# Stage boundaries of a two-block network run in two halves of 256 tokens

## The reference

```python
def first_block(x, c, ...):                  # norms after each part
    for l in range(2):
        sh1, sc1, g1, ..., g3 = split(silu(c) @ w_ada[l] + b_ada[l], 9)
        y = swiglu(modulate(x, sh1, sc1), gate, up, down)       # width 2816
        x = layer_norm(ALPHA * x + 0.5 * (1 + g1) * y)
        y = token_mixer(modulate(x, sh2, sc2), w_in, w_out)
        x = layer_norm(ALPHA * x + (1 + g2) * y)
        y = swiglu(modulate(x, sh3, sc3), gate, up, down)
        x = layer_norm(ALPHA * x + 0.5 * (1 + g3) * y)

def second_block(x, mem, ...):               # norms before each part
    for i in range(2):
        x = x + (even_mixer, odd_mixer)[i](rmsnorm(x, g_mix[i]))
        x = x + cross_attn(rmsnorm(x, g_xattn[i]), rmsnorm(mem, g_mem[i]))
        x = x + relu(rmsnorm(x, g_mlp[i]) @ w_up[i]) ** 2 @ w_down[i]   # width 4096
```

## Time and profile before

| what | us |
| --- | --- |
| median of 3 runs | 3831.74 (3830.46 to 3831.81) |
| the profiled execution | 3830.17 |
| its span, first to last instruction | 3828.9 |
| PE busy in the span | 3560.9 |
| DVE, POOL, ACT busy | 1763.9, 1426.8, 1220.7 |
| mean granted clock of PE | 0.954 |

### The profile page before, as it was taken

One profiled execution on the slowest core, in us unless ns is written; L12 is line 12 of the kernel. 1 busy time (PEld: TensorE's weight loads), 2 busy tenths in 40 slices (PEclk: granted clock), 3 DMA queues, 4 the chain that ended last, 5 costly groups with the idle time before them and its releaser, 6 DMA issues.

```text
span 3828.9 us, 41108 instructions
## 1 busy us (share of the span) xinstructions
PE 3560.9 (93%) x16548; PEld 2879.4 (75%) x16548; DVE 1763.9 (46%) x3102; ACT 1220.7 (32%) x1650; POOL 1426.8 (37%) x721
## 2 busy tenths in 40 slices
PE   8999899899998999899799988988989998988999
PEld 7888667688877888667678866746868886777888
DVE  4444654654455444644531235685552224564222
ACT  2222362332223222542332223235342232343222
POOL 3343432333344334322343342212344444525443
PEclk9999899899998999898899989978999998999999
DMA  6333321133342444211122221100212222222222
GB/s 252 143 145 134 107 88 66 72 120 139 143 143 99 143 144 142 99 66 45 65 89 95 92 83 55 56 12 34 89 59 95 99 99 71 98 69 84 91 98 77
DMA packets 52609, 373.42 MB, mean 98 GB/s; under 512 B 5826, under 2 KB 5954, under 8 KB 9539
## 3 DMA queue, kind: packets, MB, share of 16 engines
q1 hardware_dynamic: 52418, 370.79, 26.9%
HBM read 368.67 MB, written 2.10 MB: 97 GB/s over the span
## 4 chain that ended last, share of the span: by engine, by line
PE 82%; DVE 11%; ACT 3%; issue 2%; POOL 2%; DMA 0%; DVEq 0%; ACTq 0%; SPq 0%; POOLq 0%
PE ps L1213 82%; ACT s_wh L1527 1%; DVE s_nu L1808 1%; DVE s_xr L1920 1%; DVE s_tmp L1846 1%; DVE s_tmp L1843 1%; PE ps L1233 0%; ACT s_hh L1527 0%; DVE s_wl L1833 0%; DVE s_tmp L2052 0%; POOL s_hl L2314 0%; ACT s_tmp L1659 0%; DVE s_tmp L2062 0%; POOL s_wl L2321 0%; DVE s_hl L1824 0%
## 5 line engine op out<-in xcount | busy, mean ns | idle before, releaser
L2321 POOL TENSOR_TENSOR s_wl<-s_stage,s_wh 128x1024 fp32r<-128x1024 f32 (+2 forms) x277 | 925.6, 3342 | 1401.3 <-ACT s_wh L1527 1401.0
L1213 PE MATMUL ps<-s_hh,s_wh 128*128 128x512 f32 (+1 forms) x2840 | 1137.8, 401 | 66.8 <-POOL s_hl L2314 45.6
L1213 PE MATMUL ps<-s_hl,s_wh 128*128 128x512 f32 (+1 forms) x2840 | 1119.9, 394 | 0.0
L1213 PE MATMUL ps<-s_hh,s_wl 128*128 128x512 f32 (+1 forms) x2840 | 1118.7, 394 | 0.0
L1527 ACT ACTIVATE s_wh<-s_stage 128x2048 fp32r<-128x2048 f32 (+1 forms) x277 | 519.7, 1876 | 715.3 <-PE ps L1213 684.4
L1213 PEld LDWEIGHTS ps<-s_hh,s_wh 128*128 128x128 f32 (+1 forms) x2840 | 541.4, 191 | 209.2 <-issue 79.0
L1833 DVE TENSOR_TENSOR s_wl<-s_stage,s_wh 128x1024 fp32r<-128x1024 f32 (+1 forms) x268 | 328.2, 1224 | 687.1 <-ACT s_wh L1527 687.1
L1213 PEld LDWEIGHTS ps<-s_hh,s_wl 128*128 128x128 f32 (+1 forms) x2840 | 540.6, 190 | 117.3 <-issue 0.2
L1213 PEld LDWEIGHTS ps<-s_hl,s_wh 128*128 128x128 f32 (+1 forms) x2840 | 541.9, 191 | 112.7 <-issue 2.1
L1213 PE MATMUL ps<-s_ah,s_wh 128*128 128x512 f32 x1216 | 475.3, 391 | 0.0
L1213 PE MATMUL ps<-s_ah,s_wl 128*128 128x512 f32 x1216 | 474.2, 390 | 0.0
(11 more groups left out here) (408 smaller groups left out, 3660.9 us busy)
## 6 DMA issues: line engine op xcount, KB each, us to landing
s_stage<-in_w_ada SPq DMA_DIRECT2D x64, 1024.0 KB, 4.8
s_stage<-in_ffn_w_gate SPq DMA_DIRECT2D x44, 1024.0 KB, 4.8
s_stage<-in_ffn_w_up SPq DMA_DIRECT2D x44, 1024.0 KB, 4.8
s_stage<-in_ffn_down SPq DMA_DIRECT2D x32, 1024.0 KB, 4.8
s_stage<-in_w_up SPq DMA_DIRECT2D x32, 1024.0 KB, 4.8
s_stage<-in_down_m SPq DMA_DIRECT2D x32, 1024.0 KB, 4.8
s_stage<-in_w_in SPq DMA_DIRECT2D x24, 1024.0 KB, 4.8
s_stage<-in_ffn_down SPq DMA_DIRECT2D x16, 768.0 KB, 4.3
```

Source lines behind the costliest of these rows:

```text
L1213: return pe.matmul(out, lhs, rhs, start=start, stop=stop, skip_group_check=True)
L2321: pool.tensor_tensor(m.WL[:, ws, 0:cut], m.STAGE[:, j % NS, 0:cut], m.WH[:, ws, 0:cut].bitcast(F32), ALU.subtract).then_inc(*e.up("pool_w" ...
```

## The change

1. **Halves.** `residual()` takes the place of the last group's loop and of `project_out` where a norm follows: the last four chunks of down or `w_out` (two of `wo_x`) run over tokens 0 to 255 and then, with the same weights, over 256 to 511. `in_halves()` does the same with the first four chunks of the next stage. A matmul in these chunks has 256 columns, and there are twice as many. In all, 728 + 320 products of three matmuls are divided so.
2. **Norm per half.** `layer_norm` gives two generators. The first half's is a background unit during the second half of the down chunks, the second half's during the first half of the next stage. `wait_ticks` sets where its matmuls stand: mean at the second tick, variance four later, spread two later. Folds 1 and 3 of the squares go from POOL to DVE.
3. **Memory.** `NW` is 4 and `NS` 2; places 2 and 3 are lent for the feed-forward stages and boundaries and taken back in the mixers (`reclaim`). There is one `AH`/`AL`, 10 temporaries in place of 6 and a few lent ones, and `FFN_GROUPS` is (0,8), (8,6), (14,8). `whole` is gone: POOL and DVE share each chunk.
4. **Stream.** `w_ada` chunks come at a rate of 0.8 (0.7, 0.3 in places) per weight chunk, none in halved ones.
5. **Mixers.** Since four chunks are halved together, the even mixer's `index()` (top-k) starts after four chunks and not two, the odd mixer's `pool()` after four and not two, and stick-breaking after four and not three.

Lines in the changed program are other ones: L2507 is POOL's weight split, L2522 its sum over `XR`, L2501 its low part of h, L2519 the first sum; L1691 is ACT's rounding, L1733 its squares, L1742 h at full precision, L1746 the update of `XR`.

POOL at the first LayerNorm boundary, before: sums, folds of the squares, a whole split, the low parts of h.

The diff, cut to its core:

```diff
-FFN_GROUPS = [(0, 8), (8, 8), (16, 6)]
+FFN_GROUPS = [(0, 8), (8, 6), (14, 8)]
 ODD_ORDER = (4, 5, 0, 6, 1, 7, 2, 3)
 MLP_GROUPS = [(0, 8), (8, 8), (16, 8), (24, 8)]
-NS = 3
-NW = 2
+NS = 2
+NW = 4
...
+    def in_halves(self, *work, reclaim=False):
+
+        chs = []
+        for s in (0, 1):
+            if s and reclaim:
+                self.allowed = {0, 1}
+            if s and self.late:
+                self.drain(self.late)
+                self.late = None
+            for i, (name, idx, product) in enumerate(work):
+                if s == 0:
+                    if i == 0 and self.late:
+                        self.active.append(self.late)
+                    chs.append(self.take(name, idx, ada=False))
+                product(chs[i], s)
+                if s:
+                    self.release(chs[i], ("proj", self.pid))
+
+    def drain(self, unit):
+        if unit in self.active:
+            self.active.remove(unit)
+            for _ in unit:
+                pass
+
...
+    def prefetch(self):
+
+        while self.stream:
+            i = self.nsplit
+            while i < len(self.stream) and self.stream[i][2]:
+                i += 1
+            ws = [w for w in self.spare_w if w in self.allowed]
+            if i not in self.issued or not ws:
+                break
+            self.split(i, ws[0])
             self.nsplit = i + 1
 
...
+        self.due += self.rate if ada else 0
+        if self.due >= 1:
+            self.due -= 1
...
+    def lend(self, *events):
+
+        self.allowed = {0, 1, 2, 3}
+        for w in (2, 3):
+            self.wfree[w] = list(events)
...
+        def half(s):
+            yield
+            mean = self.banks.take()
+            self.add("ln_mean", sid, acc[0], mean, s)
+            if s:
+                self.tmp.free(acc[0], ("ln.mean", sid, 0), ("ln.mean", sid, 1))
+            sq = [self.tmp.take() for _ in range(4)]
+            self.add("ln_sub", sid, xv, mean, sq, s)
+            self.banks.free(mean, ("ln.sub", sid, NT - 1, s))
+            yield from self.wait_ticks(4)
+            var, y = self.held.take(), self.yr.take()
+            self.add("ln_var", sid, sq, var, y, s)
+            for q in sq:
+                self.tmp.free(q, ("ln.var", sid, s))
+            self.held.free(var, ("rs.v", "ln", sid, s))
+            yield from self.wait_ticks(2)
+            rs = self.banks.take()
+            if nxt:
+                qs = [self.tmp.take() for _ in range(4)]
+                self.add("ln_h", sid, y, rs, small, hfree[s], hv, qs, s, [v + 1 for v in xv])
+                self.yr.free(y, ("ln.rs", sid, s))
+                self.banks.free(rs, ("ln.sc", sid, NT - 1, s))
+                for i, q in enumerate(qs):
+                    self.tmp.free(q, ("h.lo", hv, 2 * i, s), ("h.lo", hv, 2 * i + 1, s))
+                if s:
+                    self.small.free(small, *both(None, "x", NT - 1, xv[NT - 1] + 1))
+                return
+            sq = [self.tmp.take() for _ in range(4)]
+            self.add("ln_last", l, idx, sid, y, rs, sq, [v + 1 for v in xv], s)
+            self.yr.free(y, ("ln.rs", sid, s))
+            self.banks.free(rs, ("ll.x", sid, NT - 1, s))
+            if s:
+                self.small.free(small, ("ln.sub", sid, NT - 1, 0))
+            yield from self.wait_ticks(4)
+            for q in sq[0:3]:
+                self.tmp.free(q, ("ll.fold", sid, 8, s))
+            yield from self.rms_half(rms[0], rms[1], rid, sq[3], packed(1), ("ll.fold", sid, 8, s), hv, hfree,
+                                     [v + 1 for v in xv], s, True)
...
+    def residual(self, names, kt, nc, x, ver, gate, norm, order=None, reads=False):
+
+        kind, begin = norm
+        total, chs, ends, per = (self.new(), []), [], [], nc // P
+        xv = [v + 1 for v in self.xv]
+        for s in (0, 1):
+            for c, (name, idx) in enumerate(names):
+                if s == 0:
+                    chs.append(self.take(name, idx, ada=False))
+                for t in range(per):
+                    n = per * c + t
+                    b, pid = self.feat(chs[c], kt, nc, t, x, ver, s, order=order)
+                    self.upd(n, xv[n], b, pid, gate, s)
+                    if n:
+                        self.total(kind, *total, n - 1, xv, s)
+                if s:
+                    self.release(chs[c], ("proj", pid))
+            self.total(kind, *total, NT - 1, xv, s)
+            ends.append(("proj", pid))
+            if s == 0:
+                if reads:
+                    self.hfree = ends
+                units = begin(total)
+                self.active.append(units[0])
+        self.drain(units[0])
+        self.late = units[1]
         if gate:
-            self.small.free(gate[-1][0], ("x", NT - 1, self.xv[NT - 1]))
-        return total if mean == "ln" else total + (("xs", total[0], NT - 1),)
-
-    def project_out(self, name, idx0, kt, nc, x, ver, gate, mean, order=None):
...
-        proj(9, "sq", True)
-        proj(10, "sk")
-        tproj(11, "sv", 0)
+        self.in_halves(("w_in", l * 12 + 9, feats("sq")), ("w_in", l * 12 + 10, feats("sk")),
+                       ("w_in", l * 12 + 11, tokens("sv", 0)), ("w_in", l * 12, feats("rq")), reclaim=True)
         self.bg.extend(sb_units())
         self.pace = 2
-        proj(0, "rq")
         proj(1, "rk")
...
+        self.in_halves(("w_kiwi", 0, keys), ("w_in_e", 7, turn_wi), ("w_in_e", 0, feats("qa", 0, 0)),
+                       ("w_in_e", 1, feats("qa", 2, 4)), reclaim=True)
...
-            self.layer_norm(l, 1, total, (l, 6, 7))
+            self.rate = 0.8
+            self.ffn("swiglu", ffn1, l, FFN_GROUPS, [2, None], then(l, 0, (l, 3, 4)))
+            self.rate = 0.3 if l == 0 else 0
+            self.first_mixer(l, then(l, 1, (l, 6, 7)))
+            self.rate = 0.8 if l else 0.7
             if l == 1:
...
-        dve.tensor_tensor(m.WL[:, ws, cut:n], m.STAGE[:, j % NS, cut:n], m.WH[:, ws, cut:n].bitcast(F32),
+        dve.tensor_tensor(m.WL[ws][:, cut:n], m.STAGE[:, j % NS, cut:n], m.WH[ws][:, cut:n].bitcast(F32),
                           ALU.subtract).then_inc(*e.up("dve_w", "w.rest", j))
...
+    def fold(sq, n, what, sid, s):
+
+        a, r = m.tmp(sq[n // 2])[:, packed(n)], m.tmp(sq[(n - 1) // 2])[:, packed(n - 1)]
+        e.wait_ge((what + ".sq", sid, n, s), (what + ".fold", sid, n - 1, s) if n in (2, 6, 7) or (what, n) == ("ll", 3) else None)
+        dve.tensor_tensor(a, a, r, ALU.add).then_inc(*e.up("dve_fold", what + ".fold", sid, n, s))
+
+    def ln_sub(sid, xv, mean, sq, s):
+        c = cols(s)
+        e.wait_ge(("ln.mean", sid, s))
         for n in range(NT):
-            e.wait_ge(xe(n, xv[n]))
-            dve.tensor_tensor(m.XR[:, n, :], m.XR[:, n, :], m.bank(mean), ALU.subtract).then_inc(
-                *e.up("dve_ln", "ln.sub", sid, n))
+            e.wait_ge(xe(n, xv[n], s))
+            dve.tensor_tensor(m.XR[:, n, c], m.XR[:, n, c], m.bank(mean)[:, c], ALU.subtract).then_inc(
+                *e.up("dve_ln", "ln.sub", sid, n, s))
+            if n in (3, 5):
+                fold(sq, n - 2, "ln", sid, s)
             if n >= 6:
-                fold(n - 1)
-        fold(7)
-
-    def ln_b(sid, y, var, rs, s, hfree, hv, qs):
-        A, B = m.small(s)[:, 0:8], m.small(s)[:, 8:16]
-        rsqrt(sid, m.bank(var)[:, 0:4], 4, 1e-5, y, ("ln.var", sid, 7))
-        e.wait_ge(("ln.rs", sid), ("ln.c", sid, 5), hfree)
+                fold(sq, n - 1, "ln", sid, s)
+        fold(sq, 7, "ln", sid, s)
```

1129 lines of the change are left out of this document (581 added, 548 removed).

## The result

The changed kernel takes 4178.6 us (4175.0 to 4183.0), the kernel before in the same session 3831.8: ratio 1.090, 95% interval 1.088 to 1.092. That is 347 us more, where the forecast said 27 less. It lies far above the range too. The profiled execution has a span of 4181.7 us.

What follows compares the result with a forecast made beforehand. PE was taken as the bound, idle mainly at norm boundaries. Boundaries −108.5, halving +42, activation buffer +5, stream +18, mixers +16 sum to −27.5 from 3828.9; with 2.8 added, 3804 us, range 3712 to 3875.

Steps and rivals of the forecast that it cites:

- the stream term: Weight stream in feed-forward stages: two stage buffers in place of three, buffer round 10.3 against PE's 10.88 us, +18 us.
- Case C: Feed-forward stages: late modulation chunks hold buffers and SP's in-order loads, starving PE; +138 in place of +18, 3924 us; chance 0.20.
- Boundaries with a LayerNorm: Norm chain partly hidden by halves: 18.4 us each, five 92 instead of 135; the last one 17 instead of 43.
- T1: End of the second half of the down chunks at a LayerNorm boundary, put 27.7 us after the first half's end.
- the place of the gap: PE waits 9.4 us at the second half's mean matmul, for POOL's running sum queued among three weight splits.
- RMS boundaries: Three boundaries without mean or folds: 2.2 us norm matmuls plus 1.3 waits, 3.5 each, 10.5 together instead of 50.
- Halving: Each split matmul costs 0.2400 in place of 0.2267 us, +0.0133; 3144 of them, +42 us, all PE's.
- One activation buffer: First matmul of nine halved or group-final down projections may wait for the last tile's low part: +5 us.
- Mixers: Top-k, pooling and stick-breaking start later; projections fill PE meanwhile, so only part shows: +16 us (0 to 30).
- something not foreseen: Sign of an unforeseen error: the mixers move by more than 30 us in either direction.
- The root's wait: LayerNorm boundary, first half: POOL's weight split holds DVE's reciprocal-root second step, so PE waits 1.9 us.

Runs made afterwards that it cites:

- the stream in order: Changed kernel, its rates kept, each modulation chunk worked off when prefetch passes it, so no weight chunk overtakes one: 3933.4 us.
- the splits behind the sums: The stream in order, plus the second half's last three down chunks at a boundary released, and so split again, only after the last sum: 3907.4 us.
- the last kernel: The stream in order and the splits behind the sums, plus the three RMS boundaries run unhalved as before the change: 3883.2 us.
- late start: Kernel before, with index/top-k and pooling units each started after four projection chunks instead of two, nothing halved: 3854.0 us, ratio 1.0053.
- MLPs halved: Kernel before, with 2976 matmuls of the two MLPs' up and down chunks each issued as two of 256 columns: 3871.1 us, ratio 1.0101.
- three placings: Kernel before, POOL's early weight split moved: right behind the last product 3836.3 us; released by the last sum 3831.6; by the last coefficient step 3817.5.
- the third placing: Kernel before, POOL's early weight split released by the last of the norm's coefficient steps at LayerNorm boundaries: 3817.5 us, ratio 0.9956.

## Why the prediction was wrong

**The step that failed is the stream term.** "Two stage buffers in place of three" was priced at +18, from the round of one buffer, 10.3 us against 10.88 of PE. Both figures hold: 10.3 is the distance of the roundings in the trace of after. What the sum didn't have is the order of loads, and taking the stream in its order gave back 245 us. Case C did name SP's in-order queue, and its sign came, waits on the weight splits and on DVE's modulation steps. But it took a steady lateness, 13.2 us a chunk and +138 in all; the stage above shows 10.3 us four times and then a gap of 30.6, 14.3 on average. It got 0.20, by the argument that "the modulation chunks are 64 in all, before and after". The order decides here, not the number: the same 64 chunks, with the same work, cost 245 us less when loads and DVE's steps go in their order. I had read the order of POOL, ACT and PE at the boundary, and not SP's in the middle of a stage, where all of it stands to be read: four modulation loads in one row.

**Boundaries with a LayerNorm.** T1 came as walked, the place of the gap too; its size was 13.5 and not 9.4, for the landing and the held sum. With the stream in order and the splits behind the sums, the first block is 26 us ahead of the kernel before at the next stage's first product, and some 11 once the second half's norm is done, its halving included. So the idea of the forecast, that a part of the chain is hidden, holds there, but for less: by the sum these six boundaries were to give 69 us, less some 29 for halving (an estimate: some 960 of the 3144 split matmuls are the RMS boundaries', by the counts of two pages, 19728 with their halves and 18768 without).

**RMS boundaries** were mis-sized: 3.5 us each, since "no mean and no folds", taken from the norm's own matmuls. They have the same weight splits in their way; one or two waits of 7 to 9 us stand at each, and undoing the halves gave 24 us, where the sum let the halves gain 39.5 less some 13 for halving.

**Halving** was right, 0.0134 (0.011 to 0.015) against 0.0133. The Trainium skill ("TensorE: Matmul & The Clock Gate", section "Back-to-back issue gap") gives an isolated matmul N/2.4 + 2.5 ns, by which a split costs 2.5 ns (the prediction wrote 2.6). For the 2976 matmuls of the MLPs that is an estimate of 7.4 us. Measured were 39.9, so for matmuls in a row here the measurement decides against it.

**One activation buffer** was right: 6.8 us of waits for its low part once the stream is in order, +5 taken. **Mixers** were mis-sized: +16 taken, and some 55 in the last kernel (48 and 22, less the norm of 15). The late start is 20 of these; the rest is mostly waits for DVE, not followed. In the changed kernel the even mixer with cross attention is 34 us longer, beyond the 30 that the prediction named as the sign of something not foreseen.

| Term | predicted | measured, and by which runs |
|---|---|---|
| stream (buffers; the order was not in the sum) | +18 | +245, the stream in order |
| splits in front of the sums | inside the 9.4 | 26, splits behind the sums |
| halves at RMS boundaries | -39.5, less their halving | +24 with halving, RMS not halved |
| halving, a matmul | 0.0133 | 0.0134, MLPs halved |
| mixers | +16 | +20 for the late start alone, late start in the kernel before; some 55 in the trace of the last kernel |

245 + 26 + 24 are 295 of the 347 us. The remaining 51 (3883.2 less 3831.8) are in the trace of that kernel -26 in the first block and +79 behind it (48, 22, 9; its span is 53.0 above, and 15 of the 48 belong to the last boundary of the first block). Of the 79, 20 are the late start; an earlier start there needs memory that is lent to the weight places, and wasn't tried.

**The root's wait.** That POOL's split holds DVE was right and is a price, though one that moves from step to step: two of three placings gained nothing in time.

## What to carry to other kernels

Where a prefetcher may overtake part of its stream, read the order of the load queue in the middle of a stage before pricing anything at its edge: with few buffers taken in turn, what was overtaken came back here in one piece. A transfer's round trip says what a steady stream costs, and nothing of a bunch. Of work on one engine that holds another, ask what stands on the other one at each place where you could put it; the third place tried here is worth 0.4%.

## What the runs showed of the hardware

The hold of DVE by POOL did not depend on the size of DVE's step: beside POOL's split of a whole chunk (4.50 us) a step of 8 columns took 4.47 us in place of 0.16, one of 512 columns 4.89 in place of 0.69. It did depend on where the step reads: in the third placing seven subtractions with one operand in PSUM ran beside the same split in 4.28 us, where they take 4.27 without it. The Trainium skill ("SBUF — State Buffer", section "SBUF: two separate sides") has the lock as exclusive for a whole instruction, and the traces agree. The earlier trace rows had shown it for one small step; I had not expected that a placing could lose at one such step nearly all that it gained at another.

Halved matmuls cost the same 0.013 us in the two MLPs (2976 of them) as the pitches of a few had shown.

PE's waits cost more here than their length: with the bunches gone PE's busy time fell by 68.5 us for the same matmuls, and the mean granted clock rose from 0.925 to 0.951.
